# Combining the differential attention's weights on GpSimd and VectorE, with three smaller moves at its scale, at the last tile's squares and at the borders

## The reference

```python
s1 = einsum('bqhd,bkhd->bhqk', a, k1) * scale        # scale = 48 ** -0.5
s2 = einsum('bqhd,bkhd->bhqk', b, k2) * scale
w = softmax(s1) - lam * softmax(s2)
o = einsum('bhqk,bkhe->bqhe', w, v)                  # then rms over the 96 values, gain, gate
```

## Time and profile before

| | |
|---|---|
| median of 3 runs | 3421.93 us (3420.61 to 3422.24) |
| profiled execution | 3425.26 us, span 3423.5 us |
| PE / PEld busy | 3210.5 us (94%) / 2532.6 us (74%) |
| DVE busy | 1682.1 us (49%) |
| ACT busy | 1212.9 us (35%) |
| POOL busy | 716.9 us (21%) |
| DMA | 260.55 MB, mean 76 GB/s |
| mean granted clock of TensorE | 0.975 of full |

### The profile page before, as it was taken

The page is one execution under the profiler, slowest core; times in us unless marked ns, Lnnn a source line. Parts: engine busy times, 40 slices in busy tenths (PEclk is TensorE's granted clock), DMA queues, the critical chain, the costliest instruction groups (busy, mean ns, idle before and its releaser), DMA issues.

```text
span 3423.5 us, 40063 instructions
## 1 busy us (share of the span) xinstructions
PE 3210.5 (94%) x16252; PEld 2532.6 (74%) x16252; DVE 1682.1 (49%) x2598; ACT 1212.9 (35%) x2068; POOL 716.9 (21%) x518
## 2 busy tenths in 40 slices
PE   6999988899988999989899899998999999989998
PEld 4777667677866788867788678886888776568886
DVE  2255565425763634457655453446444425554344
ACT  3242165434264322233344332233222325542222
POOL 3204302332513000046332300001000353230000
PEclk9999999999999999999899999999999999999999
DMA  5303200221102233222000133232232231022322
GB/s 224 117 29 111 93 30 24 64 81 53 54 24 78 80 92 105 85 89 95 19 7 1 50 102 105 96 92 81 89 109 86 80 105 44 1 81 94 109 86 80
DMA packets 77575, 260.55 MB, mean 76 GB/s; under 512 B 8400, under 2 KB 9552, under 8 KB 76240
## 3 DMA queue, kind: packets, MB, share of 16 engines
q1 hardware_dynamic: 76528, 253.28, 22.7%
q0 software_dynamic: 864, 4.72, 0.4%
HBM read 255.87 MB, written 2.10 MB: 75 GB/s over the span
## 4 chain that ended last, share of the span: by engine, by line
PE 86%; DVE 7%; ACT 3%; POOL 1%; issue 1%; DMA 1%; SPq 0%; ACTq 0%; DVEq 0%; POOLq 0%
PE banks L345 85%; PE banks L354 1%; POOL w_lo L336 1%; DVE area L576 1%; DVE small L1767 1%; DMA area<-in_w_mod 1%; DVE x_lat L579 0%; DVE area L1711 0%; ACT w_hi L326 0%; ACT area L434 0%; POOL w_late L336 0%; DVE area L1761 0%; DVE area L1749 0%; POOL area L410 0%; DVE area L494 0%
## 5 line engine op out<-in xcount | busy, mean ns | idle before, releaser
L345 PE MATMUL banks<-area,w_hi 128*128 128x512 f32 (+4 forms) x5896 | 1772.2, 383 | 26.7 <-ACT area L532 9.5
L345 PEld LDWEIGHTS banks<-area,w_hi 128*128 128x128 f32 (+2 forms) x5896 | 1080.6, 188 | 290.1 <-issue 24.3
L345 PE MATMUL banks<-area,w_lo 128*128 128x512 f32 (+4 forms) x2948 | 1121.1, 381 | 0.0
L345 PEld LDWEIGHTS banks<-area,w_lo 128*128 128x128 f32 (+2 forms) x2948 | 555.7, 189 | 119.0
L345 PE MATMUL banks<-area,w_late 128*128 128x512 f32 (+2 forms) x2316 | 579.3, 399 | 35.4 <-ACT area L532 21.1
L345 PEld LDWEIGHTS banks<-area,w_late 128*128 128x128 f32 (+1 forms) x2316 | 434.8, 190 | 152.5 <-ACT area L532 24.4
L326 ACT ACTIVATE w_hi<-w_raw 128x1024 fp32r<-128x1024 f32 (+2 forms) x361 | 349.5, 971 | 547.6 <-PE banks L345 412.8
L345 PE MATMUL banks<-area,area 128*128 128x64 f32 (+10 forms) x3896 | 473.0, 330 | 70.1 <-DMA area<-in_w_mod 16.0
L345 PEld LDWEIGHTS banks<-area,area 128*128 128x128 f32 (+4 forms) x3896 | 385.3, 184 | 157.8 <-issue 71.5
L410 POOL TENSOR_TENSOR area<-area,area 128x512 f32<-128x512 f32 (+1 forms) x102 | 140.6, 1381 | 1484.3 <-ACT area L395 1482.5
L336 POOL TENSOR_TENSOR w_lo<-w_raw,w_hi 128x1024 fp32r<-128x1024 f32 (+1 forms) x133 | 308.6, 2322 | 457.2 <-ACT w_hi L326 457.2
(11 more groups left out here) (236 smaller groups left out, 2283.7 us busy)
## 6 DMA issues: line engine op xcount, KB each, us to landing
w_raw<-in_l_ffn_w_in SPq DMA_DIRECT2D x176, 512.0 KB, 3.3
w_raw<-in_l_ffn_w_out SPq DMA_DIRECT2D x128, 384.0 KB, 3.0
w_raw<-in_w_in SPq DMA_DIRECT2D x66, 512.0 KB, 3.5
w_raw<-in_w_mod SPq DMA_DIRECT2D x32, 512.0 KB, 5.2
w_raw<-in_w_qkv SPq DMA_DIRECT2D x24, 512.0 KB, 3.3
w_raw<-in_l_w_in SPq DMA_DIRECT2D x22, 512.0 KB, 3.3
w_raw<-in_w_out SPq DMA_DIRECT2D x32, 320.0 KB, 2.9
area<-in_w_mod SPq DMA_DIRECT2D x8, 1024.0 KB, 16.6
```

The costliest lines, as they stand in the source:

```text
L345: return e.matmul(out, lhsT, rhs, start=first, stop=stop, skip_group_check=True)
```

## The change

1. *Combine.* VectorE's `combine_dve` handles only the first 256 columns, which hold the context's keys. The remaining 512 columns, the grid's keys, go to a new `combine_pool` on GpSimd, which waits for the factor, multiplies p2 by it in place, waits for that, and adds it to p1 in place. `turn_pe` waits for it ahead of the four far turns.
2. *Scale.* The factor 48 ** -0.5 is applied when ScalarE evicts the queries' projection, instead of in the exponential. The maximum is written negated by the reduction, and the multiplication behind it is gone.
3. *Last tile.* Where a stage's last output tile is not made in two halves, ScalarE squares it from the PSUM bank; VectorE's copy of that bank waits for the square.
4. *Border.* VectorE handles the first tile of the border ahead of `rest_of_weights`.

```diff
             def dve(self, q, e, after):                       # Border
-                rest_of_weights(q, e, after.first, after.LEAD - 1, dve=True)
                 for i, (s, j) in enumerate(self.tiles):
                     self.add.dve(q, e, s, j)
+                    if i == 0:
+                        rest_of_weights(q, e, after.first, after.LEAD - 1, dve=True)
...
                         q.wait_ge(*at("projected", u))        # ProjectOut.dve
+                        if self.final and m == DT - 1 and not self.add:
+                            q.wait_ge(*at(*self.squares.tag, "square", s, m))
...
-                            q.wait_ge(*at("evicted", self.group(m, s)))      # ProjectOut.act
-                            self.squares.square(q, e, s, m, self.y[:, m, c0:c1])
+                            u = self.group(m, s)
+                            if m == DT - 1 and not self.add:
+                                q.wait_ge(*at("projected", u))
+                                self.squares.square(q, e, s, m, banks[u % 4][:, 0:c1 - c0])
+                            else:
+                                q.wait_ge(*at("evicted", u))
+                                self.squares.square(q, e, s, m, self.y[:, m, c0:c1])
...
+                scale = DF_QK ** -0.5 if name == "q" else 1.0                # rope_act, both evictions
-                        e.activation(self.raw[i % 2], bank, ACT.Copy)
+                        e.activation(self.raw[i % 2], bank, ACT.Copy, scale=scale)
...
                 if self.keys(k) == TA:                                       # turn_pe
+                    q.wait_ge(*at(self.tag, "p far", k))
...
-                    e.activation(p[:, 0:n], self.scores(k)[:, w, 0:n], ACT.Exp, scale=DF_QK ** -0.5,
-                                 bias=st[:, 2 + w:3 + w], accum_out=st[:, 4 + w:5 + w])
+                    e.activation(p[:, 0:n], self.scores(k)[:, w, 0:n], ACT.Exp, bias=st[:, 2 + w:3 + w],
+                                 accum_out=st[:, 4 + w:5 + w])
...
-                e.reduce_max(st[:, 0:2], self.scores(k)[:, :, 0:self.keys(k)], X_AXIS)
-                e.tensor_scalar(st[:, 2:4], st[:, 0:2], -DF_QK ** -0.5, None, MUL)
+                e.reduce_max(st[:, 2:4], self.scores(k)[:, :, 0:self.keys(k)], X_AXIS, negate=True)
...
-                st, n = self.st(k), self.keys(k)                             # combine_dve
+                st, n = self.st(k), TC
...
+            def combine_pool(self, q, e, k):
+                st = self.st(k)
+                p1, p2 = self.p1[k % 2][:, TC:TA], self.p2[k % 2][:, TC:TA]
+                q.wait_ge(*at(self.tag, "factor", k))
+                e.tensor_scalar(p2, p2, st[:, 8:9], None, MUL).then_inc(*sig("diff_p"))
+                q.wait_ge(*last())
+                e.tensor_tensor(p1, p1, p2, ADD).then_inc(*sig("diff_p", self.tag, "p far", k))
...
                 for n in self.g_of.pieces + [out_piece]:                     # LateStage.pool
                     rest_of_weights(q, e, n)
+                for k in range(self.n):
+                    if self.keys(k) == TA:
+                        self.combine_pool(q, e, k)
```

More of the change, by code:

```diff
@@ L1501, in rope_act @@
                     if c0 >= T:
-                        e.activation(dst[:, m, c0:c1], bank, ACT.Copy).then_inc(*sig("evicted_act", "evicted", u))
+                        e.activation(dst[:, m, c0:c1], bank, ACT.Copy, scale=scale).then_inc(
+                            *sig("evicted_act", "evicted", u))
                     else:
@@ L1507, in rope_act @@
                             q.wait_ge(*at(self.tag, name, "cos", i - 2))
-                        e.activation(self.raw[i % 2], bank, ACT.Copy).then_inc(*sig("evicted_act", "evicted", u))
+                        e.activation(self.raw[i % 2], bank, ACT.Copy, scale=scale).then_inc(
+                            *sig("evicted_act", "evicted", u))
             def rope_dve(self, q, e, project, name, beside):
@@ L1696, in exp_act @@
                 for w, p in enumerate((self.p1[k % 2], self.p2[k % 2])):
-                    e.activation(p[:, 0:n], self.scores(k)[:, w, 0:n], ACT.Exp, scale=DF_QK ** -0.5,
-                                 bias=st[:, 2 + w:3 + w], accum_out=st[:, 4 + w:5 + w]).then_inc(
+                    e.activation(p[:, 0:n], self.scores(k)[:, w, 0:n], ACT.Exp, bias=st[:, 2 + w:3 + w],
+                                 accum_out=st[:, 4 + w:5 + w]).then_inc(
                         *sig("diff_exp", self.tag, "exp", k, w))
@@ L1766, in max_dve @@
                 q.wait_ge(*at(self.tag, "s", k))
-                e.reduce_max(st[:, 0:2], self.scores(k)[:, :, 0:self.keys(k)], X_AXIS).then_inc(*sig("softmax"))
-                q.wait_ge(*last())
-                e.tensor_scalar(st[:, 2:4], st[:, 0:2], -DF_QK ** -0.5, None, MUL).then_inc(
+                e.reduce_max(st[:, 2:4], self.scores(k)[:, :, 0:self.keys(k)], X_AXIS, negate=True).then_inc(
                     *sig("softmax", self.tag, "max", k))
             def combine_dve(self, q, e, k):
-                st, n = self.st(k), self.keys(k)
+                st, n = self.st(k), TC
                 p1, p2 = self.p1[k % 2][:, 0:n], self.p2[k % 2][:, 0:n]
@@ L1779, in combine_dve @@
                 e.scalar_tensor_tensor(st[:, 8:9], st[:, 4:5], lam_cols[self.l][:, 3:4], st[:, 7:8], MUL, MUL).then_inc(
-                    *sig("softmax"))
+                    *sig("softmax", self.tag, "factor", k))
                 q.wait_ge(*last())
                 e.scalar_tensor_tensor(p1, p2, st[:, 8:9], p1, MUL, ADD).then_inc(*sig("softmax", self.tag, "p", k))
+            def combine_pool(self, q, e, k):
[5 more added lines that the diff above has]
+                e.tensor_tensor(p1, p1, p2, ADD).then_inc(*sig("diff_p", self.tag, "p far", k))
             def pool(self, q, e, out_piece):
```

## The result

The changed kernel takes 3433.72 us (median of 6 runs, 3432.28 to 3437.72) against 3422.00 of the kernel before on the same chip: ratio 1.0037 (95% interval 1.0025 to 1.0049). It is 11.7 us slower; the forecast was 3422.5, with a range to 3431. The profiled execution took 3434.67 us, its span is 3432.9, 9.4 above the span of before.

What follows compares the result with a forecast made beforehand. TensorE, 86% of the span, was taken as the bound, so other engines count only where it waits. Loops +10.9, last tile -2.0, first tile -8.3 gave +0.6: 3422.5 us, range 3412 to 3431, forecast as no change.

Steps and rivals of the forecast that it cites:

- The combination at full clock: Both attention loops: far turns wait for GpSimd's late sum; layer 0 +6.4 us, layer 1's step 4.84 instead of 4.61.
- blocked and unblocked: Loops: whether or not GpSimd and VectorE block each other, the total hardly moves; only who is late differs.
- layer 0's +1.73 per head: Layer 0's loop: steps grow by 0.71, 0.18, 0.74 and 0.18, two others by -0.08 and 0.
- rival (c): Loops: GpSimd gets in before VectorE's near part, +1.4 us per step in layer 1, 3444 in all; chance 0.04.
- rival (b): Layer 0's loop: TensorE's clock falls to half once per head, 2.5 x 4 = 10 us, 3432 in all; chance 0.12.
- Layer 1: Layer 1's loop: +3.1 us from first to last o, and +1.4 ahead of it for a slower start.
- Scale and maximum: Attention loops: taken as 0; one VectorE operation less lets the factor start 0.08 us earlier, -0.08 at one step per head.
- Last tile and first tile: Stage borders: last tile 0.6 to 0.75 us at three, -2.0; first tile 2.08 at four FFN borders, -8.3.
- rival (d): Borders: TensorE runs dry or the gain is given back, -5 rather than -10 us, 3428 in all; chance 0.07.
- (a): Loops: GpSimd is in time, layer 1 unchanged, layer 0 -1 us, only the borders' gain left, 3411; chance 0.12.

Runs made afterwards that it cites:

- kernel with six turns: Changed kernel plus six needless 128x128 turns ahead of the wait for GpSimd, only in layer 0's two long waits per head: 3426.89 us, ratio 1.0012.
- run 1: Changed kernel with the combination of all 768 columns back on VectorE, the other edits kept: 3407.81 us, ratio 0.9960.
- run 12: Kernel before with only the combination's far columns moved to GpSimd: 3438.47 us, ratio 1.0043.

## Why the prediction was wrong

*The combination at full clock: right, by compensating errors.* The kernel with six turns shows it without the half clock. Its loop in layer 0 is 5.1 us longer than before; forecast 6.4. A head takes 26.6 where 26.9 were forecast. But 2.2 of saving by scale and maximum are in this (below): against run 1 the same loop is 7.3 longer, and that is what the combination costs there at full clock. Layer 1's step is 4.80; forecast 4.84. The delay sits elsewhere, too. I had norm stand still until GpSimd's scaling ended, so the VectorE-bound steps would grow by 0.7 and the far turns be only 0.18 late. In fact norm takes 0.70 and ends 0.8 ahead of the scaling (1010.87 against 1011.68); the step of 4.18 became 3.79 and the one of 3.93 kept its length. The far turns' wait then falls whole on the following steps: 4.87 to 6.0 and 4.18 to 5.0. The prediction said that blocked and unblocked differ in who is late and hardly in the sum; that held (per head +0.71 +0.18 +0.74 +0.18 -0.1 forecast, -0.4 +1.1 0 +0.8 0 found, and -0.1 at the 256-key step).

The Trainium skill, SBUF — State Buffer, section "Who interferes with whom", which the prediction names at rival (c), has the later of two contending engines stand still for the whole of the earlier one's instruction. For GpSimd behind the near part the trace comes close: the near part runs on for 0.43 behind the scaling's start, which lengthens the scaling by 0.29. For norm behind the scaling it doesn't agree: 0.70, 0.43 more than its usual 0.27, and not the 1.5 to the scaling's end. The measurement decides.

*The failed step: "TensorE's clock falls in the loop", left out of layer 0's +1.73 per head and given a chance of 0.12.* This is rival (b), and it came on top of the waits. Between the changed kernel (113.40) and the one with six turns (101.92) it is worth 11.5 us; (b) said 10. That the two agree so well is in part luck: (b) counted four falls of 2.5; the trace has three that cost 5.8 (over three steps), 2.9 and 1.6, and 1.2 in the loop's last step, and with the same lulls the clock can also stay up (run 12). It fell where (b) put it, behind the leanest step of layer 0. What I did wrong was the weight I gave it. The rows were there: TensorE busy 2.83 of 4.18 at full clock, already with lulls of 0.5 and 0.6 in it. I let the clock of 1.00 before speak for 1.00 after, though the forecast itself added a wait to that very place. With (b) taken in, the forecast would have been 3422.5 + 10 = 3432.5.

The Trainium skill, TensorE: Matmul & The Clock Gate, section "HAM oscillation — how this bites in real kernels", describes waits between short pieces of work that make each next piece start at the lower clock. The trace agrees in kind, 0.90 us of idleness and then 0.50 of the clock, but its wait is several times shorter than the ones described there, and the next piece doesn't start low each time (8 of 12).

*Layer 1.* Its loop costs 3.4 against run 1 (forecast 3.1), but shows only +0.4 against before, since before ended that loop with steps of 5.94 and 6.65 at half clock, and after with 4.99 and 5.28. At its start the delay is 2.8, forecast 1.4: there TensorE's 24 matmuls ran at half clock too (4.43 us at 993.35; 3.30 before, and 3.08 in run 1).

*Scale and maximum: priced 0, worth 2.2 in layer 0.* The multiplication sat on VectorE, and its end with it: in layer 1's step the combination starts 2.11 behind the maximum's start instead of 2.30. I took 0.08 for these 0.19, and carried it into one step per head; the steps of 4.18, 4.18 and 3.38 became 3.88, 3.98 and 3.28, 0.6 per head.

*Last tile and first tile: right at the border, less sure in the sum.* 0.8 and 2.0 at the first border alone, 2.85 together (forecast 0.67 + 2.08). Behind layer 1 the gain is 9.6 in all (forecast 10.3), but that number also holds what the clock did in the recurrent mixer (last section), so its closeness is partly luck. Of rival (d) there was some: the 93 lead matmuls of the first border last 24.4 us (1125.10 to 1149.48) instead of 23.74, and the first tile alone gave 3.0 of its 8.6 back in the FFNs behind the borders. Rivals (a) and (c) didn't occur: the steps are not all 4.61, and the near part stayed at 0.48.

## What to carry to other kernels

Where a change adds a wait to TensorE, add up the lulls of that step, not only the wait: here a new wait of 0.9 us cost 1.1 as a wait, and as clock up to 2.9 in the same step and 5.8 with the two behind it. Such a fall is told from contention by putting needless matmuls into the lull: if the steps behind it come back to their length, it was the clock. Read it from the steps; the program's time also holds what the turns cost and what the clock does elsewhere. At a place where another engine sets the pace, the same trick gives nothing. And an engine that has nothing to do is no place for work whose result TensorE wants at once: only as much as it has done in time is free.

## What the runs showed of the hardware

- GpSimd's 128x512 scaling by a column takes 1.56 with nothing on VectorE, 1.64 beside a norm that started ahead of it, and 1.85 behind 0.48 us of VectorE's two-input work; 256 columns 1.48 behind 0.75 us of it. Its sum of two 128x512 tiles takes 1.26 every time here.
- The same work can run at either clock far from any edit. The recurrent mixer has the same 2688 matmuls in all kernels. As one window, before, and in the kernel with scale and maximum alone:

```profile
1493.00:1941.50 448.50, 410.31 (x2688) 341.73 (x2688) 269.19 (x442) 170.51 (x265) 190.17 (x117) 0.94 0.12 40
```

```profile
1485.30:1924.00 438.70, 400.83 (x2688) 331.58 (x2688) 269.13 (x442) 170.38 (x265) 190.63 (x117) 0.96 0.12 41
```

  Nothing is changed in it, yet TensorE is busy 9.5 us less and the window is 9.8 us shorter. Among the kernels with the changed borders, the stretch from the border ahead of it to the one behind differs from before by -3.1 to -12.5 us. So edits of a few microseconds don't add up in this program, and a difference of under some 10 us has to be read stage by stage. What decides in which execution this stage runs faster stays open.
- At the same place of the loop and with the same lulls ahead of it, the clock fell once in three times in the kernel with the combination alone: a lull of 0.90 us made the fall possible there and did not force it, and with the lull filled the clock fell in none of nine such places.
